# Attention over 64-feature heads: two heads in turn on halves of the TensorE array, turned rows copied by ScalarE

## The reference, cut to what matters

```
# EA, layer 0: 8 query heads, 2 key heads, a band of 128 tokens, a sink, softmax
s = q @ k.T * 64**-0.5 + bias          # per head and block of 128 queries
m = max(s, sink);  p = exp(s - m);  p = p / (sum(p) + exp(sink - m));  o = p @ v
# EB, layer 0: 8 heads, causal, stick-breaking
z = q @ k.T * 64**-0.5
a = sigmoid(z) * prod over later keys of sigmoid(-z);  o = a @ v
# OC, layer 1: 16 heads, causal, softmax with a table of biases per head (3 dilations joined)
# SX, third block: 16 query heads, 4 key heads, causal, softmax over the keys that an index chose
```

## Time and profile before

| | |
|---|---|
| three runs | 3391.88, 3394.07, 3395.95 us |
| the profiled execution: time, span of its instructions | 3395.51 us, 3393.7 us |
| TensorE busy, mean granted clock | 3284.9 us of the span (97%), 0.975 |
| DVE, ACT, POOL busy | 1454.8, 1157.3, 220.9 us |
| EA: first score to last value product | 494.5 to 539.4 us |
| EB | 539.3 to 618.6 us |
| OC | 1726.6 to 1830.5 us |
| SX | 2805.8 to 2911.9 us |

### The profile page before, as it was taken

One profiled execution on the slowest core, in us unless ns is written; L12 is line 12 of the kernel. 1 busy time (PEld: TensorE's weight loads), 2 busy tenths in 40 slices (PEclk: granted clock), 3 DMA queues, 4 the chain that ended last, 5 costly groups with the idle time before them and its releaser, 6 DMA issues.

```text
span 3393.7 us, 36847 instructions
## 1 busy us (share of the span) xinstructions
PE 3284.9 (97%) x14548; PEld 2627.4 (77%) x14548; DVE 1454.8 (43%) x2354; ACT 1157.3 (34%) x1887; POOL 220.9 (7%) x439
## 2 busy tenths in 40 slices
PE   8999998999999999999999999999999999989998
PEld 6888775777788888887866877888887785768887
DVE  3332337554333243323555543332325766543332
ACT  3232334343322133223344533332226624332221
POOL 1000100010000000000400100000132100010000
PEclk9999998999999999999999999999989999989999
DMA  4322220231332323332312412333222230223331
GB/s 140 100 94 99 87 81 1 87 124 50 93 100 94 99 89 96 96 100 87 99 59 66 138 50 86 95 93 100 73 87 75 73 109 5 75 71 97 100 100 68
DMA packets 212605, 291.44 MB, mean 86 GB/s; under 512 B 13872, under 2 KB 135984, under 8 KB 212304
## 3 DMA queue, kind: packets, MB, share of 16 engines
q1 hardware_dynamic: 209792, 279.59, 26.3%
q0 software_dynamic: 2640, 9.50, 0.9%
HBM read 286.94 MB, written 2.10 MB: 85 GB/s over the span
## 4 chain that ended last, share of the span: by engine, by line
PE 90%; DVE 5%; ACT 3%; POOL 1%; issue 1%; DMA 0%; POOLq 0%; DVEq 0%; ACTq 0%
PE ps L94 87%; PE ps L97 3%; DVE ebQ L115 1%; DVE hTl L109 0%; ACT xn L100 0%; POOL stat L103 0%; DVE ebP L103 0%; ACT L100 0%; DVE ebPT L121 0%; DVE s_ri L115 0%; POOL s_ri L103 0%; DVE xn L106 0%; ACT wh L100 0%; POOL e_ss L103 0%; ACT hTh L100 0%
## 5 line engine op out<-in xcount | busy, mean ns | idle before, releaser
L103 DVE TENSOR_TENSOR wl<-raw,wh 128x1024 fp32r<-128x1024 f32 (+1 forms) x530 | 640.9, 1216 | 1249.5 <-ACT wh L100 1244.4
L100 ACT ACTIVATE wh<-raw 128x1024 fp32r<-128x1024 f32 (+1 forms) x530 | 552.4, 1051 | 1362.0 <-PE ps L94 1318.2
L94 PE MATMUL ps<-hTh,wh 128*128 128x512 f32 x2144 | 841.1, 392 | 16.6 <-DVE hTl L109 16.6
L94 PE MATMUL ps<-hTl,wh 128*128 128x512 f32 x2144 | 838.1, 391 | 0.0
L94 PE MATMUL ps<-hTh,wl 128*128 128x512 f32 x2144 | 837.6, 391 | 0.0
L94 PEld LDWEIGHTS ps<-hTh,wh 128*128 128x128 f32 x2144 | 404.9, 189 | 104.4 <-DVE hTl L109 13.7
L94 PEld LDWEIGHTS ps<-hTl,wh 128*128 128x128 f32 x2144 | 405.1, 189 | 84.7 <-issue 1.0
L94 PEld LDWEIGHTS ps<-hTh,wl 128*128 128x128 f32 x2144 | 404.9, 189 | 84.8
L94 PE MATMUL ps<-wh,hTh 128*128 128x512 f32 (+2 forms) x832 | 324.2, 390 | 10.0 <-DVE hTl L109 5.8
L94 PE MATMUL ps<-wl,hTh 128*128 128x512 f32 (+2 forms) x832 | 321.4, 386 | 0.0
L94 PE MATMUL ps<-wh,hTl 128*128 128x512 f32 (+2 forms) x832 | 321.4, 386 | 0.0
(11 more groups left out here) (347 smaller groups left out, 4076.1 us busy)
## 6 DMA issues: line engine op xcount, KB each, us to landing
raw<-in_ffn_w_gu SPq DMA_DIRECT2D x352, 256.0 KB, 3.1
raw<-in_ffn_w_down SPq DMA_DIRECT2D x88, 512.0 KB, 3.5
raw<-in_xa_w_kv SPq DMA_DIRECT2D x32, 512.0 KB, 4.0
raw<-in_w_in SPq DMA_DIRECT2D x32, 512.0 KB, 3.7
raw<-in_od_w_in SPq DMA_DIRECT2D x24, 512.0 KB, 3.6
raw<-in_w_ffn_gate SPq DMA_DIRECT2D x44, 256.0 KB, 2.9
raw<-in_w_ffn_up SPq DMA_DIRECT2D x44, 256.0 KB, 3.1
raw<-in_w_ffn_down SPq DMA_DIRECT2D x22, 512.0 KB, 3.8
```

Source lines behind the costliest of these rows:

```text
L94: return self.made(lambda e: e.matmul(*a, **k))
L100: return self.made(lambda e: e.activation(*a, **k))
L103: return self.made(lambda e: e.tensor_tensor(*a, **k))
```

## The change

Heads are worked on in pairs. Step s now gives scores to both heads of pair s, transposes pair s-1 and multiplies pair s-2 with v. The score matmuls of the two heads alternate, one on partitions 0 to 63 and one on 64 to 127 (the halves of the array's rows), and so do the value products, one to output partitions 0 to 63 and one to 64 to 127 (the halves of its columns). Each group of rows has a score bank per head (`sbank`: four banks, the slots alternate from group to group), three banks take the transposes in rotation (`tbank`), one bank (7) the values. The causal groups are rows [3], [2, 0], [1], those of the band [2, 3], [1, 0]. Reciprocals and the sink's addition are done once per pair. `PT` has one buffer per head of the pair. ACT alone copies the turned rows. EB's DVE waits for the ones before it adds the mask, and POOL fills four buffers. The third block's buffers are placed elsewhere. `Whole` holds what the cross attention did before, in the order that it had.

The diff, cut to its core:

```
+CAUSAL_GROUPS = [[3], [2, 0], [1]]
+BAND_GROUPS = [[2, 3], [1, 0]]
...
+        def sbank(self, s, n, u):
+            return 2 * ((s * len(self.groups) + n) % 2) + u
+        def tbank(self, s, u, n):
+            return 4 + ((2 * s + u) * len(self.groups) + n) % 3
...
+    def pe_pairs(pe, A, qT, kT, qkey, kkey, kv_of, V, vkeys):
+        def scores(s):
...
+            for n, group in enumerate(A.groups):
+                for u in range(2):
+                    b = A.sbank(s, n, u)
+                    pe.wait_ge(drained, pe.held[b])
+                    pe.held[b] = (A.tag, s, "s", n, u)
+                parts = [list(A.scores(s, n, u)) for u in range(2)]
+                for both in zip(*parts):
+                    for u, (i, W, dst) in enumerate(both):
+                        k0, k1, _, _ = A.spans[i]
+                        r = slice(64 * u, 64 * u + 64)
+                        ins = pe.matmul(dst, qT[r, s, i * P:(i + 1) * P], kT[r, kb, k0 * P:k1 * P], start=True, stop=True)
+                        if i == group[-1]:
+                            ins.then_inc(scored, (A.tag, s, n, u))
+        def turn(s):
+            for u in range(2):
+                for n, group in enumerate(A.groups):
+                    b, at = A.tbank(s, u, n), 0
+                    pe.wait_ge(drained, pe.held[b])
...
+        def values(s):
...
+                for kt in range(NT):
+                    for u in range(2):
+                        ins = pe.matmul(o_[64 * u:64 * u + 64, kt * P:S], V(2 * s + u, kt), A.pt[u][:, kt, kt * P:S],
+                                        start=kt == 0, stop=kt == NT - 1)
...
+        for s in range(A.N + 2):
+            if s < A.N:
+                scores(s)
+            if s >= 2:
+                values(s - 2)
+            if 1 <= s <= A.N:
+                turn(s - 1)
...
+    def act_pairs(act, A, O, base_, gone):
...
+        for s in range(A.N + 2):
+            if s < A.N:
+                (sigmoids if A.stick else exps)(s)
+            if s >= 2:
+                act.wait_ge(valued, (A.tag, s - 2))
+                act_hi(act, bank[VBANK][:, :], O, base_ + s - 2, slice(0, S), gone)
+            if 1 <= s <= A.N:
+                for u in range(2):
+                    for n, group in enumerate(A.groups):
+                        act.wait_ge(turned, (A.tag, s - 1, n, u))
+                        if s >= 2:
+                            act.wait_ge(valued, (A.tag, s - 2))
+                        put_turned(act, A.pt[u], bank[A.tbank(s - 1, u, n)], A.spans, group, (A.tag, s - 1, n, u)).also(
+                            drained, (A.tag, s - 1, "t", n, u))
+    def dve_pairs(dve, A, O, base_, bias=None):
+        def first(s):
+            for n, group in enumerate(A.groups):
+                for u in range(2):
...
+                    for i, W, src in A.scores(s, n, u):
+                        ins = dve.tensor_tensor_reduce(A.row(s, u, i), src, bias(2 * s + u, i, W), 1.0, FLOOR, ALU.add,
+                                                       ALU.max, mx[:, i:i + 1])
+                    ins.then_inc(maxed, (A.tag, s, n, u)).also(drained, (A.tag, s, "s", n, u))
...
+        if A.stick:
+            dve.wait_ge(ones_set, A.tag)
+        for s in range(A.N + 2):
+            if s < A.N:
+                (before if A.stick else first)(s)
+            if 1 <= s <= A.N:
+                (breaks if A.stick else later)(s - 1)
+            if s >= 2:
+                dve.wait_ge(valued, (A.tag, s - 2))
+                dve_lo(dve, bank[VBANK][:, :], O, base_ + s - 2, slice(0, S)).also(drained, (A.tag, "o", s - 2))
...
-            pool.memset(EB.q[b][:, :], 1.0).then_inc(ones_set, "eb")
+            for u in range(2):
+                pool.memset(EB.q[b][u][:, :], 1.0).then_inc(ones_set, "eb")
```

More of the change, by code:

```diff
@@ L696, in dve_turned, with put_turned @@
             ins.then_inc(put, (name, g, "T", c)).also(drained, ("turn", name, g, c))
[L699 to L708, removed]
-            if self.stick:
[L710 to L716, removed]
+    def put_turned(e, dst_of, src, spans, group, done):
+        at = 0
+        for i in group:
+            k0, k1, _, W = spans[i]
+            s_ = src[:, at:at + W].rearrange("p (k q) -> p k q", k=k1 - k0)
+            d_ = dst_of[:, k0:k1, i * P:(i + 1) * P]
+            ins = e.activation(d_, s_, AF.Copy) if e.name == "act" else e.tensor_copy(d_, s_)
+            at += W
+        return ins.then_inc(put, done)
@@ L718, in small, with __init__ @@
+    class Whole:
+        groups = [[0, 1], [2, 3]]
+        def __init__(self, tag, H, area, scale):
+            self.tag, self.H, self.scale = tag, H, scale
+            self.p = [sb(f"{tag}P{i}", [P, WHOLE_W], F32, area) for i in range(2)]
+            self.pt = [sb(f"{tag}PT{i}", [P, 2, S], F32, area) for i in range(2)]
+            self.sm = [sb(f"{tag}sm{i}", [P, 16], F32, area) for i in range(2)]
         def small(self, h, i):
             return self.sm[h % 2][:, 4 * i:4 * i + 4]
-        def sbank(self, h, n):
-            return n if self.causal else 2 * (h % 2) + n
@@ L724, in scores @@
[L724 to L748, removed]
-            if s < A.H:
[L750 to L761, removed]
-            if 1 <= s <= A.H:
[L763 to L778, removed]
-                for n, group in enumerate(A.groups):
[L780 to L832, removed]
@@ L838, in put_turned @@
             e.wait_ge(valued, (A.tag, h - 2))
[L839 to L848, removed]
@@ L938, in act_pair_out @@
[L938 to L950 removed]
+        put_turned(e, A.pt[h % 2], bank[4 + n], WHOLE, A.groups[n], (A.tag, h, n)).also(drained, (A.tag, h, "t", n))
@@ new lines, in act_whole @@
+    def act_whole(act, A, finish):
+        for s in range(A.H + 3):
+            if s >= 3:
+                finish(s - 3)
+            if s < A.H:
+                nm, den = A.small(s, 1), A.small(s, 2)
+                act.wait_ge(maxed, (A.tag, s))
+                if s >= 2:
+                    act.wait_ge(turned, (A.tag, s - 2, 1))
+                for i in range(NT):
+                    ins = act.activation(A.row(s, i), A.score(s, i), AF.Exp, bias=nm[:, i:i + 1], scale=A.scale,
+                                         accum_out=den[:, i:i + 1])
+                    if i % 2:
+                        ins.then_inc(drained, (A.tag, s, "s", i // 2)).also(expd, (A.tag, s))
+            if 1 <= s <= A.H:
+                whole_turned(act, A, s - 1, 0)
@@ new lines, in dve_whole @@
+    def dve_whole(dve, A, finish):
+        for s in range(A.H + 3):
+            if 1 <= s <= A.H:
+                den, rd = A.small(s - 1, 2), A.small(s - 1, 3)
+                dve.wait_ge(expd, (A.tag, s - 1))
+                dve.reciprocal(rd, den).then_inc(step, (A.tag, s - 1, "r"))
+                dve.wait_ge(step, (A.tag, s - 1, "r"))
+                for i in range(NT):
+                    dve.tensor_scalar(A.row(s - 1, i), A.row(s - 1, i), rd[:, i:i + 1], None, ALU.mult).then_inc(
+                        normed, (A.tag, s - 1, i))
+            if s < A.H:
+                mx, nm = A.small(s, 0), A.small(s, 1)
+                for n, group in enumerate(A.groups):
+                    dve.wait_ge(scored, (A.tag, s, n))
+                    if s >= 2:
+                        dve.wait_ge(turned, (A.tag, s - 2, 1))
+                    for i in group:
+                        ins = dve.tensor_reduce(mx[:, i:i + 1], A.score(s, i), AX, ALU.max)
+                    ins.then_inc(maxed, (A.tag, s, n))
+                dve.wait_ge(maxed, (A.tag, s, 1))
+                dve.tensor_scalar(nm, mx, -A.scale, None, ALU.mult).then_inc(maxed, (A.tag, s))
+            if s >= 3:
+                finish(s - 3)
+            if 1 <= s <= A.H:
+                whole_turned(dve, A, s - 1, 1)
@@ L1544, in value @@
                 ins.then_inc(valued, (A.tag, h, c)).also(valued, (A.tag, h))
-        pe_attend(pe, A, score, value)
+        pe_whole(pe, A, score, value)
     def act_cross(act, C):
```

307 lines of the change are left out of this document (176 added, 131 removed).

## The result

The changed kernel takes 3400.79 us (median of 15 runs, 3399.16 to 3402.37), the kernel before 3392.81 (15 runs beside it, 3391.11 to 3395.95). The ratio is 1.0023, 95% interval 1.0015 to 1.0031: slower by 8.0 us, just over the 0.2% (7 us) that the prediction called no change. The profiled execution took 3399.7 us with a span of 3397.9. It lies 1.1 us under its median and that of the kernel before 2.7 over, so the two traces differ by 4.2 us of the 8.0.

The account below looks back on a forecast made before the run. OC and SX, bound by TensorE, would become bound by a chain of waits worsened by the low clock. Stage changes of +1.7, +1.4, +0.7 and -1.6 give +2.2, 3396.3 us; 0.7 for hand-overs makes 3397, range 3368 to 3418.

Parts of the forecast that it names:

- low clock at each turn: Rival, chance 0.32: the chain meets the low clock every turn, 13.9 us each; OC +8.9, SX +6.6, EA and EB +3; 3415.
- Row and column halves run together: Score and value matmuls of a pair's two heads overlap on TensorE; value products of a pair take 2.3 us, not 4.6.
- OC's chain of 11.5 us at the high clock: In OC, waits through scores, maxima, eight exponentials, copies and transposes sum to 11.5 us per pair at 2.4 GHz.
- The mean turn of 12.6 to 12.7: In OC, the clock falling in some turns lifts the 11.5 us per pair to 12.6 to 12.7; stage 104.5 us.
- the sum: Changes of the four stages added: EA +1.7, EB +1.4, OC +0.7, SX -1.6, together +2.2 us.
- a sign of being right: In OC, starts of pairs' first scores were to lie 12 to 13.5 us apart.
- EA: Stage EA: 10.1 us per pair at the high clock, 46.6 us with the low clock, against 44.9: +1.7.
- EB: Stage EB: DVE's copies go but new waits come; 17.1 us per pair at the low clock, stage 80.6 us: +1.4.
- the wait for the last scores that I priced: In EB, DVE's mask additions wait for a pair's last scores, whose banks four sigmoids must drain first (2.1 us).
- the clock stays up: Rival, chance 0.2: TensorE keeps the high clock; EA 41, EB 73, OC and SX 93.8 us; 32 us less, 3362.
- column halves apart: Rival, chance 0.08: value products take 4.6 us per pair, fill TensorE's gap and keep the clock up; 17 less, 3377.
- ACT's evacuation as the bound: Rival, chance 0.01: ACT's 7.6 us of work per pair bounds OC; 30 us less per stage, about 3325.

## Why the prediction was right or wrong

The forecast was 3397 us, range 3368 to 3418; measured were 3400.8. The view of the whole was right: the halves of the array give OC and SX nothing, because a new chain takes TensorE's place as the bound and the clock takes what is left. That the number came so close is luck in part. The stages' errors have both signs (+4.3 in OC and +6.3 in SX, -3.9 in EA and -2.1 in EB), and what OC and SX do is the mechanism of the rival "low clock at each turn", which had a chance of 0.32 and a time of 3415.

- **Row and column halves run together**: right. A pair's value products took 2.38 us; 2.3 was taken. By "TensorE: Matmul & The Clock Gate", Part 3, of the Trainium skill, column tiles overlap; this trace agrees, and the run with the heads not in turn adds that they did so fully only when issued in turn (3.93 us otherwise).
- **OC's chain of 11.5 us at the high clock**: right, 11.48 with the clock held up. Its eight exponentials took 4.37 (4.4), the copies 1.38 (1.4).
- **The mean turn of 12.6 to 12.7**: the term that was wrong. I expected the low clock to fall now on the chain and now beside it. The first turn was 12.59. From the second on the clock fell in each one, always on the second head's transposes and the first scores, since the gap ahead of it is part of the same ring (filled, it kept the clock up): 13.6 us. Five turns took 66.95 us (1739.13 to 1806.08), 13.4 each, for 63.5; the stage's end took 25.5 for 24.4; OC came out at 108.8 for 104.5. SX, forecast the same, took 110.9, some 2 us more than OC as in the kernel before. That is +5.0 and +4.7 where the sum had +0.7 and -1.6. Four of the five turns are also just over the 13.5 us that the prediction gave as a sign of being right.
- **EA**: forecast +1.7, measured -2.2. Its start was right (13.64 us to the third pair's scores, for 13.9), a turn was 10.6 for 11.3, and the end 18.5 for 21.4: the 4 us for the low clock there were too many.
- **EB**: forecast +1.4, measured -0.7. First scans 18.6 us in (19.5), turn 16.67 (17.1). The reason was partly wrong: the wait for the last scores that I priced is 0.65 of the 4.7 us of waits. The rest is for the pair's first scores, and the low clock is a part of that: in the turn with the largest waits, holding it up with the masks moved took 1.2 us off the first and 0.8 off the second. What DVE's copies are worth, 10.4 us in the kernel before, stood in no term by itself.
- **Rival "the clock stays up"**: the clock held up gives 3382.0 and not 3362. Its turn was right, but OC's ends were not: 97.9 us for 93.8, and SX took 100.5. That run doesn't test all of the rival: EB had no fill and kept its 0.72 (78.0 us for 73), and in EA the fill itself cost time (45.5 for 41).
- **Rival "column halves apart"**: they weren't apart in the changed kernel. With products that mostly don't overlap (3.93 us) its mechanism came as described, at 3387.0 for 3377.
- **Rival "low clock at each turn"**: this is what OC and SX do, though their mean clock is 0.75 in a turn and not near 0.55. Its condition, a mean turn over 13.0, is met with 13.4, but its price was too high: turns of 13.6 for 13.9 (the terms given add up to 14.0), and EA and EB gained where it gave them 3 us more each. With its turns at 13.6 (five in each of two stages, 3 us less) and EA and EB at zero (6 less) it would have given 3406.
- **Rival "ACT's evacuation as the bound"**: excluded by the same time for the two kernels with different loads. The Trainium skill, "TensorEngine Tiling (Array Packing)", Performance Considerations, asks for both ScalarE and VectorE when emptying PSUM. Here both engines gave 3346.9 and ACT alone in a better order 3347.0, so what counted was what stands ahead of the copies.

Not settled: why the clock, with a gap of 1.7 us, fell in one turn of OC and not in the others; and how EB's 16.67 us would divide if its clock alone were held up with the masks left in place, which wasn't tried.

## What to carry to other kernels

When a change halves one engine's work, look for the ring of waits that takes its place and for what stands ahead of its releasing instruction in that engine's program: here the order of ACT's exponentials and copies was worth 54 us in the three softmax stages, and which engine did the copies was worth nothing there (in EB, bound by DVE, it was worth 10). Where a ring contains an idle stretch of TensorE, ask whether the clock falls in it and what comes next; if that is on the ring, count the low clock in every turn and not in some (here it was four of five turns, at 13.6 us for 11.5). A few matmuls that nobody reads show what the clock costs, and may be kept where they fit into the gap; in EA, where they didn't, they cost 2.8 us.

## What the runs showed of the hardware

- Faster matmuls can make a kernel slower: value products of 2.38 us for a pair instead of 3.93 left a gap of 3.40 us instead of mostly 1.7, the clock fell in each turn of OC from the second on instead of in one of five, and the kernel took 3400.8 us instead of 3387.0.
- Column halves of the array ran fully together only with the two heads' products issued in turn (2.38 us for both, as for one; 3.93 head by head). Row halves didn't need that (2.00 and 2.10 us for the first twelve score matmuls), where each group has at most four matmuls per head.
- Matmuls put into TensorE's gap in OC (3.17 us in each turn) kept the granted clock at 1.00 through 80 us of the stage; without them it was at 0.50 for half of a turn (6.9 of 13.6 us).
